# Two output units of a projection computed side by side while the input is still being prepared

## The reference, cut to what matters

```
xn   = x * rsqrt(mean(x*x) + 1e-6) * norm1          # pre-norm, D_MODEL = 1024
proj = xn @ w_in                                     # 1024 -> 2560 columns
rc, q, k, v = split(proj)                            # RWKV-7 part and attention part
q, k = rms_norm per head
o    = concat(rwkv7(rc), sliding_window_attention(q, k, v))
h    = x + o @ w_out
y    = h + square(relu(rms_norm(h) @ w_up)) @ w_down
```

## Time and profile before

| | |
|---|---|
| median of 3 runs | 1636.96 us (1635.55 to 1637.64) |
| the profiled execution | 1637.65 us |
| its span in the profile | 1635.9 us |
| TensorE matmul busy | 1519.7 us, 93% of the span |
| projection | from the start to 282.6 us |

### The profile page before, as it was taken

One profiled execution on the slowest core, in us unless ns is written; L12 is line 12 of the kernel. 1 busy time (PEld: TensorE's weight loads), 2 busy tenths in 40 slices (PEclk: granted clock), 3 DMA queues, 4 the chain that ended last, 5 costly groups with the idle time before them and its releaser, 6 DMA issues. The chain is left out here.

```text
span 1635.9 us, 37435 instructions
## 1 busy us (share of the span) xinstructions
PE 1519.7 (93%) x15843; PEld 1435.8 (88%) x15843; DVE 729.3 (45%) x1211; ACT 589.2 (36%) x1225; POOL 132.0 (8%) x155
## 2 busy tenths in 40 slices
PE   6999999699989889569999999999999999999998
PEld 5999999577777777369988999999999999999998
DVE  6123333566666666351253444433344433334444
ACT  6443111466656655531134222233222223322211
POOL 3000000222222222300000000000000000000000
PEclk9999999799999999779999999999999999999999
DMA  6111110100000000141011111111011111111003
GB/s 185 44 48 39 38 51 0 33 4 4 3 4 3 4 3 5 33 129 65 26 52 52 52 52 51 28 51 51 26 51 51 38 38 51 42 35 51 26 0 110
DMA packets 81989, 66.78 MB, mean 41 GB/s; under 512 B 14385, under 2 KB 73963, under 8 KB 81867
## 3 DMA queue, kind: packets, MB, share of 16 engines
q1 hardware_dynamic: 79963, 64.42, 13.3%
q10 hardware_dynamic: 1840, 0.53, 0.1%
q0 software_dynamic: 64, 0.03, 0.0%
HBM read 59.59 MB, written 5.44 MB: 40 GB/s over the span
## 5 line engine op out<-in xcount | busy, mean ns | idle before, releaser
L102 PE MATMUL bank<-mix_hi,uw_hi 128*128 128x384 f32 (+1 forms) x768 | 252.9, 329 | 6.6 <-DVE uw_lo L1982 6.6
L102 PE MATMUL bank<-u_hi,dw_hi 128*128 128x384 f32 (+1 forms) x768 | 253.0, 329 | 5.9 <-DVE dw_lo L1987 3.6
L2002 DVE TENSOR_TENSOR hT<-hT,bank 128x384 f32<-128x384 f32 (+1 forms) x384 | 195.0, 529 | 131.3 <-PE bank L104 131.2
L104 PE MATMUL bank<-mix_hi,uw_lo 128*128 128x384 f32 (+1 forms) x768 | 252.8, 329 | 0.0
L103 PE MATMUL bank<-mix_lo,uw_hi 128*128 128x384 f32 (+1 forms) x768 | 252.7, 329 | 0.0
L103 PE MATMUL bank<-u_lo,dw_hi 128*128 128x384 f32 (+1 forms) x768 | 251.2, 327 | 0.0
L104 PE MATMUL bank<-u_hi,dw_lo 128*128 128x384 f32 (+1 forms) x768 | 251.1, 327 | 0.0
L1994 DVE TENSOR_TENSOR u_lo<-xn,u_hi 128x384 fp32r<-128x384 f32 (+1 forms) x96 | 51.5, 536 | 302.4 <-ACT u_hi L1953 302.4
L102 PE MATMUL bank<-x_hi,w_hi 128*128 128x384 f32 (+1 forms) x480 | 160.2, 334 | 0.1
L103 PE MATMUL bank<-x_lo,w_hi 128*128 128x384 f32 (+1 forms) x480 | 158.5, 330 | 0.0
L104 PE MATMUL bank<-x_hi,w_lo 128*128 128x384 f32 (+1 forms) x480 | 158.4, 330 | 0.0
(11 more groups left out here) (268 smaller groups left out, 2545.4 us busy)
## 6 DMA issues: line engine op xcount, KB each, us to landing
w_stage<-in_w_up SPq DMA_DIRECT2D x32, 512.0 KB, 4.5
d_stage<-in_w_down SPq DMA_DIRECT2D x32, 512.0 KB, 4.3
w_stage<-in_w_in SPq DMA_DIRECT2D x16, 512.0 KB, 3.8
proj<-in_x SPq DMA_DIRECT2D x9, 512.0 KB, 5.4
xs<-in_x SPq DMA_DIRECT2D x9, 512.0 KB, 5.0
w_stage<-in_w_in SPq DMA_DIRECT2D x8, 256.0 KB, 4.3
w_stage<-in_w_out SPq DMA_DIRECT2D x8, 256.0 KB, 3.1
w_stage<-in_w_out SPq DMA_DIRECT2D x16, 128.0 KB, 3.4
```

The source lines that it names most:

```text
L102: pe.matmul(out, hi, x_hi, start=first, stop=False)
L104: return pe.matmul(out, lo, x_hi, start=False, stop=last)
L2002: dve.tensor_tensor(hT[:, m, c:c + n], hT[:, m, c:c + n], bank[j % 6][:, 0:n], ALU.add).then_inc(dn_add.sem, 1)
```

## The change

Three things change, all in `phase_project`.

- **The order on PE.** Units 0 and 1 are computed side by side, group by group: turn 0 to 3; unit 0 group 0; turn 4 and 5; unit 1 group 0; turn 6; first half of unit 0 group 1; turn 7; second half; turn 8; unit 1 group 1; unit 0 group 2; unit 1 group 2. The first two groups of unit 1 signal on a semaphore of their own (`early_full`), and the last one raises `acc_full` by 3.
- **The transposes on two banks.** All tiles are turned into banks 6 and 7, the first four transposes into bank 6 and the other four into bank 7, since unit 1 now needs banks 3 to 5 early. `turn(t)` waits for each half of `x_gain(t - 1)`, not for `x_gain(t - 2)`; and `x_gain` waits for each half of the transposes, not for all eight. The small jobs move from bank 3 to bank 5.
- **The first weights.** `hi` and `lo` of units 0 and 1 move from t = 4 and 6 to t = 3 and 5.

```
-                    if t in (4, 6):
-                        hi(t // 2 - 2, t // 2 - 2)
+                    if t in (3, 5):
+                        hi(t // 2 - 1, t // 2 - 1)
...
                 def x_gain(t):
-                    dve.wait_ge(x_turned.sem, x_turned.n(t))
                     for h in range(2):
-                        src = bank[4 + 2 * (t % 2) + h][:].rearrange("p (k c) -> p k c", k=4)
+                        dve.wait_ge(x_turned.sem, x_turned.n(t, h))
+                        src = bank[6 + h][:].rearrange("p (k c) -> p k c", k=4)
...
-                    if t in (4, 6):
-                        lo(t // 2 - 2, t // 2 - 2)
+                    if t in (3, 5):
+                        lo(t // 2 - 1, t // 2 - 1)
...
                 def turn(t):
                     pe.wait_ge(x_scaled.sem, x_scaled.n(t))
-                    if t >= 2:
-                        pe.wait_ge(x_gained.sem, x_gained.n(t - 2, 1))
-                    for k in range(KT):
-                        mm = pe.transpose(bank[4 + 2 * (t % 2) + k // 4][:, P * (k % 4):P * (k % 4) + P],
-                                          x_scl[t % 2][:, P * k:P * k + P], ident[:])
-                    mm.then_inc(x_turned.sem, 1)
+                    for h in range(2):
+                        if t >= 1:
+                            pe.wait_ge(x_gained.sem, x_gained.n(t - 1, h))
+                        for k in range(4):
+                            mm = pe.transpose(bank[6 + h][:, P * k:P * k + P], x_scl[t % 2][:, P * (4 * h + k):P * (4 * h + k) + P], ident[:])
+                        mm.then_inc(x_turned.sem, 1)
...
-                for t in range(1, 6):
+                for t in range(1, 4):
                     turn(t)
...
                 pe.wait_ge(wlo_ok.sem, wlo_ok.n(0))
                 pe.wait_ge(xlo_ok.sem, xlo_ok.n(2))
-                product(0, 0, 0, range(0, 4))
+                product(0, 0, 0, range(KT)).then_inc(acc_full.sem, 1)
+                turn(4)
+                turn(5)
+                pe.wait_ge(wlo_ok.sem, wlo_ok.n(1))
+                product(1, 1, 0, range(KT)).then_inc(early_full.sem, 1)
                 turn(6)
-                product(0, 0, 0, range(4, 8)).then_inc(acc_full.sem, 1)
+                pe.wait_ge(xlo_ok.sem, xlo_ok.n(5))
+                product(0, 0, 1, range(0, 4))
                 turn(7)
+                product(0, 0, 1, range(4, 8)).then_inc(acc_full.sem, 1)
                 turn(8)
-                for g in (1, 2):
-                    pe.wait_ge(xlo_ok.sem, xlo_ok.n(3 * g + 2))
-                    product(0, 0, g, range(KT)).then_inc(acc_full.sem, 1)
+                product(1, 1, 1, range(KT)).then_inc(early_full.sem, 1)
+                pe.wait_ge(xlo_ok.sem, xlo_ok.n(8))
+                product(0, 0, 2, range(KT)).then_inc(acc_full.sem, 1)
                 pe.wait_ge(bvec_c.sem, bvec_c.n(0))
-                for pos in range(1, FIRST):
+                product(1, 1, 2, range(KT)).then_inc(acc_full.sem, 3)
+                head_sums(0)
+                for pos in range(2, FIRST):
                     unit(pos, pos % 2)
```

More of the change, by code:

```diff
@@ L142, in phase_project @@
         x_sq, x_ln, x_rstd, x_scaled = sem("x_sq"), sem("x_ln"), sem("x_rstd"), sem("x_scaled")
-        x_turned, x_gained = sem("x_turned"), sem("x_gained", 2)
+        x_turned, x_gained = sem("x_turned", 2), sem("x_gained", 2)
         xhi_ok, xlo_ok = sem("xhi_ok"), sem("xlo_ok")
@@ L146, in phase_project @@
         whi_ok, wlo_ok = sem("whi_ok"), sem("wlo_ok")
-        acc_full, acc_read = sem("acc_full", 3), sem("acc_read", 3)
+        acc_full, early_full, acc_read = sem("acc_full", 3), sem("early_full"), sem("acc_read", 3)
         d_ok, d_fix, mixed = sem("d_ok"), sem("d_fix"), sem("mixed")
@@ L238, in evac @@
                     for g, (c, n) in enumerate(GROUPS):
-                        act.wait_ge(acc_full.sem, acc_full.n(pos, g))
+                        if isinstance(pos, int) and pos == 1 and g < 2:
+                            act.wait_ge(early_full.sem, early_full.n(g))
+                        else:
+                            act.wait_ge(acc_full.sem, acc_full.n(pos, g))
                         act.activation(proj[:, bass.ds(u, 1), c:c + n].rearrange("p a n -> p (a n)") if not isinstance(u, int)
@@ L270, in _ @@
                     if t >= 2:
-                        act.wait_ge(x_turned.sem, x_turned.n(t - 2))
+                        act.wait_ge(x_turned.sem, x_turned.n(t - 2, 1))
                     act.activation(x_scl[b], x_tok[t % NX], ACT.Square, accum_out=stat[:, t:t + 1]).then_inc(x_sq.sem, 1)
@@ L280, in _ @@
                         x_upper(t - 2)
-                    if t in (4, 6):
-                        hi(t // 2 - 2, t // 2 - 2)
+                    if t in (3, 5):
+                        hi(t // 2 - 1, t // 2 - 1)
                     if t == 4:
                         act.wait_ge(bvec_t.sem, bvec_t.n(0))
-                        act.activation(vec, bank[3][0:8, 0:208], ACT.Copy).then_inc(bvec_c.sem, 1)
+                        act.activation(vec, bank[5][0:8, 0:208], ACT.Copy).then_inc(bvec_c.sem, 1)
                 x_upper(NT - 2)
@@ L365, in _ @@
                         dve.wait_ge(par_t.sem, par_t.n(0))
-                        dve.tensor_copy(par[:], bank[3][:, 0:NROW]).then_inc(par_ok.sem, 1)
+                        dve.tensor_copy(par[:], bank[5][:, 0:NROW]).then_inc(par_ok.sem, 1)
                         dve.wait_ge(par_ok.sem, par_ok.n(0))
@@ L432, in _ @@
                 pe.wait_ge(rows_in.sem, 16)
-                pe.transpose(bank[3][:, 0:NROW], rows[0:NROW, :], ident[0:NROW, 0:NROW]).then_inc(par_t.sem, 1)
-                for t in range(1, 6):
+                pe.transpose(bank[5][:, 0:NROW], rows[0:NROW, :], ident[0:NROW, 0:NROW]).then_inc(par_t.sem, 1)
+                for t in range(1, 4):
                     turn(t)
[L436 to L440, removed]
+                pe.wait_ge(b_in.sem, 32)
+                pe.wait_ge(par_ok.sem, par_ok.n(0))
+                pe.matmul(bank[5][0:8, 0:208], rel, onehot, start=True, stop=True).then_inc(bvec_t.sem, 1)
                 pe.wait_ge(wlo_ok.sem, wlo_ok.n(0))
                 pe.wait_ge(xlo_ok.sem, xlo_ok.n(2))
-                product(0, 0, 0, range(0, 4))
+                product(0, 0, 0, range(KT)).then_inc(acc_full.sem, 1)
[3 more added lines that the diff above has]
+                product(1, 1, 0, range(KT)).then_inc(early_full.sem, 1)
                 turn(6)
-                product(0, 0, 0, range(4, 8)).then_inc(acc_full.sem, 1)
+                pe.wait_ge(xlo_ok.sem, xlo_ok.n(5))
+                product(0, 0, 1, range(0, 4))
                 turn(7)
+                product(0, 0, 1, range(4, 8)).then_inc(acc_full.sem, 1)
                 turn(8)
-                for g in (1, 2):
-                    pe.wait_ge(xlo_ok.sem, xlo_ok.n(3 * g + 2))
-                    product(0, 0, g, range(KT)).then_inc(acc_full.sem, 1)
+                product(1, 1, 1, range(KT)).then_inc(early_full.sem, 1)
+                pe.wait_ge(xlo_ok.sem, xlo_ok.n(8))
+                product(0, 0, 2, range(KT)).then_inc(acc_full.sem, 1)
                 pe.wait_ge(bvec_c.sem, bvec_c.n(0))
-                for pos in range(1, FIRST):
+                product(1, 1, 2, range(KT)).then_inc(acc_full.sem, 3)
+                head_sums(0)
+                for pos in range(2, FIRST):
                     unit(pos, pos % 2)
```

## The result

The changed kernel took 1643.88 us (median of 15 runs, 1636.77 to 1649.63), the kernel before 1637.92 us (median of 15, 1632.68 to 1643.58). The ratio is 1.0032, 95% interval 1.002 to 1.0044: **slower by 0.32%, about 5.2 us (3.3 to 7.2)**; the two medians by themselves are 6.0 us apart. The forecast was 1638.7 us and "within 0.2%"; both the time and the class are missed, on the side of rival 2 and beyond its 1641.2 us.

The account below looks back on a forecast made before the run. PE was dense from 42.07 us, so only its start-up counted: the start gains 4.2 us, the way to the head sums grows 5.95 us, net +1.75 us on 1636.96 gives 1638.7 us; range 1635.4 to 1641.4.

Parts of the forecast that it names:

- rival 2: Clock falls in the new pause between first and second group product: +3.4 to +4.3 us, 1640.3 to 1641.2 us; chance 13%.
- The method of the mark: Change in the start of the first head sums (54.16 us before), units 0 and 1 complete, equals change in time.
- The early start: PE starts unit 0's first product at 20.65 us instead of 24.86 us, 4.2 us earlier.
- the cover for `hi(0)`: On ACT, `hi(0)` (1.04 us) ends at 16.2 us, inside the wait for tile 4 until 16.55 us, costing nothing.
- The first product: Unit 0's group 0 on PE takes 5.35 us (4.6 to 6.7), with 13 matmuls at the lower clock.
- The two pauses: PE waits 2.65 us before unit 1's group 0 for `w_lo`, and 2.3 us after `turn(6)` for `x_lo`.
- The last stretch: From unit 0's group 1 to the head sums PE is dense: 6.0 us, then three groups in 12.5 us.
- `lo(2)` of unit 2: Ends with the other preparing steps while PE does the head sums: hidden, with 1.9 us to spare.
- the 0 for the two banks: Finer handshakes at the transposes in tiles 1 to 3 change nothing: 0, bounds 0.4 us either way.
- the 0.9 us for turn 5: If the clock falls in the new pause, turn 5 on PE costs up to 0.9 us more.
- the chain on DVE: At t = 5, `x_gain(4)`, `x_lower(3)` and `lo(1)` take 1.27 + 1.22 + 1.22 us, delaying unit 1's group 0.
- the base of the forecast: Median time taken for the kernel before, 1636.96 us, to which +1.75 us was added.

## Why the prediction was wrong

**What held.** The method of the mark: in the first profile the projection after it is the same to 0.01 us. The early start at 20.54 us (20.65 predicted; 21.67 and 21.16 us in the other two), and the cover for `hi(0)`: it ran at 15.15 us and the squares of tile 4 at 16.10 us, without a wait. The first product took 5.55 us (5.35; 5.25 and 6.41 in the other two). The two pauses, their places and their releasers; the second took 3.18 us with its turn (3.2). The last stretch took 18.54 us (6.0 + 12.5). `lo(2)` of unit 2 ended before the head sums did. Nothing speaks against the 0 for the two banks: alone, their mark came 0.9 us earlier, which is outside the 0.4 us allowed for, but this is the earlier landing of tile 4, and the interval of the time includes zero.

**What failed, first: the choice between the forecast and rival 2.** The step was "transposes of this size keep the clock. Chance 13%". The rival's conditions and price were right (5.32 - 3.74 = 1.6 us, as it said; the 0.9 us for turn 5 did not come, it ran at the high level), its chance was not: the clock fell at the first pause in 4 of 4 profiles, and at the second, to which I gave no chance at all, in 3 of 5. What I had weighed was a dense row of 48 transposes at the end. It says that transposes in a dense row keep the clock. It does not say that two turns with holes and then 2.53 us of nothing do, and the row that resembled the case, a pause of 2.24 us with thin work around it, pointed to a fall. By the experiments with idle work and with the moved steps the pauses are the cause of the falls, at about 1.5 us each. My estimate from these counts is 1.5 + 0.6 x 1.5 = 2.4 us in an execution.

The rule of the Trainium skill, "TensorE: Matmul & The Clock Gate", Part 4, that transposes do not count as busy for the clock gate in the way matmuls do, was on the side of the fall. Yet it is not shown to be the reason. In two of the three profiles of the changed kernel turn 3 ran at the high level (1.10 us for eight transposes at 15.57 us, 1.09 us at 16.69 us) before any product had been computed, so transposes alone had raised the clock; in the third it took 1.97 us. That speaks against the rule as it is put.

**Second: a term mis-sized.** "the three take 1.27 + 1.22 + 1.22 us" for the chain on DVE; the last took 2.02 us in the changed kernel (and 2.02 us in its second profile), so unit 1's product started 5.24 us after turn 4 and not 4.45. The late turn had moved `lo(1)` beside POOL's scaling of tile 6. With `lo(1)` made earlier it took 1.23 us, with POOL idle. In all six profiles in which `lo(1)` started beside POOL's scaling it took 2.02 to 2.04 us, in the four of versions in which it did not 1.22 or 1.23 us. That the two slow each other is thus seen by their place in seven versions, but POOL alone was not moved. In the rows shown above it is the one that started second that takes longer. The Trainium skill, "GPSIMD Engine Reference", section 1, says that POOL's paths to SBUF are shared with VectorE and contend with its instructions of two SBUF inputs, which `lo` is; 2.02 against 1.22 us agrees.

**The sum again.** 55.9 predicted, less 0.1 for the start, plus 0.2 for the first product, 0.8 for `lo(1)` and 1.6 for the clock is 58.4 us, the mark of the first profile. The other two had 60.6 and 59.9 us. The mean of the three is 59.6 us, 3.7 us above the prediction: 0.5 for the start, 0.4 for the first product, 0.8 for `lo(1)`, 1.5 for the clock at the first pause and 0.5 for the clock at the second. The kernel before has 54.3 us in the mean of two, so the mark moved by +5.3 us, and the time measured is +5.2 us (3.3 to 7.2). With marks that spread over 2.2 us an agreement to 0.1 us is luck, but no loss behind the mark is needed. Another 1.0 us of the missed time is in the base of the forecast, 1636.96 us for the kernel before, which has 1637.92 us in 15 runs.

**What of it is chance.** The first profile's span grew by 7.5 us, 3.3 more than its mark. Windows of the second half of the kernel show where it lies: the clock falls or holds at waits that the change does not touch. First the kernel before, then the changed kernel, from 840 to 850 us and later, PE alone (its time busy, instructions, clock, DMA share and GB/s):

```profile
840.00:850.00 10.00, 9.04 (x57) 1.00 0.66 209
870.00:880.00 10.00, 10.00 (x53) 0.83 0.65 210
```

```profile
840.00:850.00 10.00, 7.30 (x26) 0.68 0.42 120
870.00:880.00 10.00, 6.10 (x26) 0.72 0.32 93
```

The changed kernel lost its clock in a wait of 2.67 us that ended at 844.29 us; the kernel before kept it in the same wait of 2.67 us, which ended at 840.97 us. But the second profile of the kernel before shows 0.68 from 840 to 850 us too, and the second and third of the changed kernel 1.00. It goes both ways and is scatter, not a consequence that these runs can show. It also bears on the forecast: this wait, behind several microseconds of dense work, stands in all 14 profiles with 2.67 us and cost the clock in 5 of them, against 4 of 4 for the slightly shorter one behind two thin turns. The length of a pause alone does not decide.

**What the change gave and took.** The whole change with its turns moved gives 4.9 us (2.1 to 7.5) over the kernel before; what the interleaving alone gives of it was not measured. The change had the start, and lost all of it and more because it queued turns 4 and 6, already ready, behind whole group products, while DVE's next work hung on them. It takes both orders, PE's and DVE's, for the pauses: with either of them altered they are gone or under 0.5 us.

## What to carry to other kernels

When a new order fills an engine's idle time, list for each preparing step that it delays who waits for it, in that engine's own program order. Work that is ready and short goes ahead of long work if a chain on other engines starts from it. And a new pause of 2 us in front of dense matmuls is to be priced with the clock's fall, here 1.5 us, times how often it falls at pauses of that kind: it was 4 of 4, 3 of 5 and 5 of 14 at three places in this kernel. One row of one profile in which the clock held is not enough to put the price at nothing.

## What was not expected of the hardware

- At pauses of 2.53 us after two turns with gaps the granted clock dropped in 4 of 4 profiles, at pauses of 2.15 us in 3 of 5, and at a wait of 2.67 us behind dense work in 5 of 14. In two of the first four it dropped 1.0 and 1.1 us after dense work had begun again. Behind the 2.53 us the high level was back 3.0 to 4.4 us after the start of the product. The same 2.5 us with twelve matmuls in them and 0.7 us left empty kept the clock in both profiles.
- Transposes alone raised the clock, in some executions: turn 3 of the changed kernel took 1.10 us for eight in one profile and 1.97 us in another, with no product before either. The kernel before took 1.97 us at the same point. The column of granted clock does not tell these apart, it reads 1.00 there in all of them.
- A subtraction on DVE with both inputs in SBUF took 2.02 us instead of 1.22 beside POOL's scaling of a tile of the same size that had started 0.22 us earlier. Where DVE had started 0.34 us earlier, it took 1.22 us and POOL 1.87 us instead of 1.12.
